# Pick steps dealt out anew, and six expert dots of units 8 and 9 on TensorE in place of five GpSimd products

## The reference, cut to what matters

```python
def peer_ffn(h, w_q, sub_keys, u_tab, v_tab):
    q = (xt @ w_q).reshape(n, PEER_HEADS, 2, PEER_QDIM // 2)
    s = jnp.einsum("nhpd,hpkd->nhpk", q, sub_keys)
    s1, i1 = lax.top_k(s[:, :, 0], PEER_TOPK)
    s2, i2 = lax.top_k(s[:, :, 1], PEER_TOPK)
    ...
    top_s, pos = lax.top_k(cand_s, PEER_TOPK)
    experts = jnp.take_along_axis(cand_i, pos, axis=-1)
    g = jax.nn.softmax(top_s, axis=-1)
    a = jax.nn.gelu(jnp.einsum("td,thkd->thk", xc, u_tab[ec]))
    return jnp.einsum("thk,thkd->td", gc * a, v_tab[ec])
```

## Time and profile before

| | us |
|---|---|
| median of 3 runs | 2062.68 (2062.55 to 2067.21) |
| profiled execution | 2062.78, span 2061.5 |
| early stage, first to last VectorE dot | 771.2 to 1304.5 |
| units 8 to 11 of it | 1134.6 to 1304.5 |
| spreading tile 1's coefficients | 1304.5 to 1339.0 |
| value stage | 1339.0 to 2061.5 |
| TensorE, VectorE, ScalarE, GpSimd busy | 1817.1, 1537.4, 868.2, 522.0 |

### The profile page before, as it was taken

The page is one execution under the profiler, slowest core; times in us unless marked ns, Lnnn a source line. Parts: engine busy times, 40 slices in busy tenths (PEclk is TensorE's granted clock), DMA queues, the critical chain, the costliest instruction groups (busy, mean ns, idle before and its releaser), DMA issues.

```text
span 2061.5 us, 28478 instructions
## 1 busy us (share of the span) xinstructions
PE 1817.1 (88%) x11068; PEld 1622.3 (79%) x11068; DVE 1537.4 (75%) x2053; ACT 868.2 (42%) x1347; POOL 522.0 (25%) x426
## 2 busy tenths in 40 slices
PE   6999999999999999957775244599999999999997
PEld 6999999999999887856775134488888888888886
DVE  5464444334465548999999989977888889999997
ACT  5444444444433441122332778534433444334443
POOL 0000000001044003433333577012121214443431
PEclk9999999999999999978898556799999999999999
DMA  9566555655466879999999899388999999999995
GB/s 313 160 169 174 163 163 169 174 166 164 143 181 218 312 252 419 380 423 384 394 384 396 305 427 427 124 310 332 417 400 386 401 376 378 407 395 405 397 409 187
DMA packets 293542, 627.87 MB, mean 305 GB/s; under 512 B 10364, under 2 KB 223405, under 8 KB 234958
## 3 DMA queue, kind: packets, MB, share of 16 engines
q0 software_dynamic: 48400, 343.95, 41.8%
q1 hardware_dynamic: 244558, 282.20, 40.0%
q10 hardware_dynamic: 496, 0.58, 0.1%
HBM read 622.45 MB, written 8.44 MB: 306 GB/s over the span
## 4 chain that ended last, share of the span: by engine, by line
PE 67%; DVE 16%; DVEq 7%; issue 4%; DMA 3%; POOL 2%; ACT 1%; SPq 0%; POOLq 0%; ACTq 0%
PE ps L1867 34%; PE ps L1553 23%; DVE u_ring L1398 7%; DVEq L1353 6%; PE ps L1733 4%; DMA u_ring<-in_peer_u,idx_all 2%; PE ps L1719 1%; POOL u_ring L667 1%; PE ps L1658 1%; PE ps L1639 1%; DVE ones L1430 1%; DVE ones_d L1430 1%; PE ps L1648 1%; DVE pick L1386 0%; DVE key_all L1389 0%
## 5 line engine op out<-in xcount | busy, mean ns | idle before, releaser
L1161 DVE TENSOR_TENSOR w_lo<-raw,w_hi 128x2048 fp32r<-128x2048 f32 x112 | 259.1, 2313 | 327.2 <-ACT w_hi L718 327.1
L1553 PE MATMUL ps<-act_hi,w_hi 128*128 128x256 f32 x1536 | 442.3, 288 | 4.8 <-DVE act_lo L1286 2.9
L1553 PE MATMUL ps<-act_hi,w_lo 128*128 128x256 f32 x1536 | 436.4, 284 | 0.0
L1553 PE MATMUL ps<-act_lo,w_hi 128*128 128x256 f32 x1536 | 436.4, 284 | 0.0
L1098 ACT ACTIVATE v_hi<-v_raw 128x2048 fp32r<-128x2048 f32 x128 | 245.5, 1919 | 404.0 <-PE ps L1867 211.4
L1867 PE MATMUL ps<-v_hi,c_hi 128*128 128x512 f32 x1024 | 404.6, 395 | 2.2 <-DVE c_lo L1481 2.2
L1867 PE MATMUL ps<-v_hi,c_lo 128*128 128x512 f32 x1024 | 403.2, 394 | 0.0
L1867 PE MATMUL ps<-v_lo,c_hi 128*128 128x512 f32 x1024 | 401.1, 392 | 0.0
L1398 DVE CUSTOM_DVE_ANT_0 u_ring<-u_ring,ps 128x2048 f32<-128x2048 f32 x156 | 353.9, 2277 | 21.4 <-DMA u_ring<-in_peer_u,idx_all 21.0
L1479 DVE TENSOR_TENSOR v_lo<-v_raw,v_hi 128x2048 fp32r<-128x2048 f32 x128 | 293.1, 2290 | 68.6 <-ACT v_hi L1098 67.5
L718 ACT ACTIVATE w_hi<-raw 128x2048 fp32r<-128x2048 f32 x112 | 214.1, 1911 | 266.8 <-PE ps L1553 222.0
(11 more groups left out here) (234 smaller groups left out, 2154.0 us busy)
## 6 DMA issues: line engine op xcount, KB each, us to landing
v_raw<-in_peer_v SPq DMA_DIRECT2D x128, 1024.0 KB
raw<-in_w_in SPq DMA_DIRECT2D x80, 1024.0 KB
raw<-in_w_out SPq DMA_DIRECT2D x16, 1024.0 KB
wq<-in_peer_w_q SPq DMA_DIRECT2D x8, 2048.0 KB, 12.7
raw<-in_w_br_a SPq DMA_DIRECT2D x16, 512.0 KB
bias_by_query<-bias_by_distance POOLq DMA_DIRECT2D x1, 4096.0 KB, 20.4
bias_st<-bias_by_query POOLq DMA_DIRECT2D x16, 256.0 KB, 4.7
raw<-in_w_br_b SPq DMA_DIRECT2D x16, 256.0 KB
```

Of the source, the lines that this page charges most:

```text
L1161: nc.vector.tensor_tensor(w_lo[:, j % NHL], raw[:, j % NRAW], w_hi[:, j % NHL].bitcast(F32), ALU.subtract).then_inc(lo_done, 1)
L1553: last = nc.tensor.matmul(out_ap, w_parts[wp][:, slot, k], act_parts[ap][:, k], start=(k == k0 and m == 0), stop=(k == k1 - 1 and m == 2))
```

## The change

It does four things.

1. **Six dots to TensorE.** In units 8 and 9 the picks (8, 1), (8, 5), (8, 9), (9, 0), (9, 4), (9, 8) (`PE_LATE`) go the way (c). The five picks there that GpSimd multiplied, (8, 7), (8, 12), (9, 2), (9, 7), (9, 12), go back to VectorE. All these late dots use PSUM banks 4 and 5 alone, since banks 0 to 3 hold the token rows: transposes alternate between the two, and the product goes into bank 4. So a late dot's transposes wait until VectorE has taken the diagonal of the dot before, the product waits for the third copied group, and ScalarE copies into one buffer (`rows_u`), where before there were two.
2. **Pick steps.** Unit 7 gets 18 steps in place of 26 and none in its last five picks, unit 8 gets 8 in place of 16 and only in its last six picks, unit 9 gets 16 in place of none.
3. **Coefficient groups.** ScalarE builds 21 in place of 18, seven in unit 8 (before 5), seven in unit 9 (before 5), six in unit 10 and one in unit 11. VectorE builds 11 in place of 14, none before unit 10, since their buffer lies over `xgT`, which the late dots read.
4. **Small things.** The identity scaled by the norm, by which the diagonal is taken, exists for both tiles; `slot_order` counts on a late TensorE dot's slot one pick later.

```diff
--- before.py
+++ after.py
@@ -86,10 +86,9 @@
 GROUPS = P // GTOK
 WQ_AT = (0, 16, 64, 80, 32, 48, 0, 16)
 WQ_TURN = tuple(WQ_AT[:u + 1].count(kib) for u, kib in enumerate(WQ_AT))
-ACT_GROUP_AT = {(8, 3): 0, (8, 5): 1, (8, 8): 2, (8, 11): 3, (8, 14): 4, (9, 1): 5, (9, 4): 6, (9, 7): 7, (9, 10): 8, (9, 13): 9,
-                (10, 1): 10, (10, 4): 11, (10, 7): 12, (10, 10): 13, (10, 13): 14, (11, 1): 15, (11, 3): 16, (11, 6): 17}
-DVE_GROUP_AT = {(9, 11): 0, (10, 0): 1, (10, 1): 2, (10, 5): 3, (10, 6): 4, (10, 10): 5, (10, 11): 6, (10, 15): 7,
-                (11, 1): 8, (11, 5): 9, (11, 6): 10, (11, 10): 11, (11, 11): 12, (11, 12): 13}
+ACT_GROUP_AT = {at: n for n, at in enumerate([(8, k) for k in (3, 4, 6, 8, 10, 12, 14)] + [(9, k) for k in (0, 2, 4, 7, 9, 11, 14)]
+                                             + [(10, k) for k in (0, 3, 5, 8, 11, 13)] + [(11, 1)])}
+DVE_GROUP_AT = {at: n for n, at in enumerate([(10, k) for k in (0, 1, 5, 6, 10, 11, 15)] + [(11, k) for k in (1, 5, 6, 10)])}
 ACT_GROUPS, DVE_GROUPS = len(ACT_GROUP_AT), len(DVE_GROUP_AT)
 W_INC = 48
 RING = 4
@@ -107,17 +106,20 @@
 
 
 EARLY = [(u, k) for u in range(N_EARLY) for k in range(PTOP)]
-STEPS_BY_UNIT = {0: 13, 1: 16, 2: 20, 8: 16, 9: 0, 10: 0, 11: 0}
+STEPS_BY_UNIT = {0: 13, 1: 16, 2: 20, 7: 18, 8: 8, 9: 16, 10: 0, 11: 0}
 
 
 def on_pool(u, k):
 
-    return u >= PH and k in (2, 7, 12) and (u, k) not in ((8, 2), (11, 12))
+    return u >= PH + 2 and k in (2, 7, 12) and (u, k) != (11, 12)
+
+
+PE_LATE = ((8, 1), (8, 5), (8, 9), (9, 0), (9, 4), (9, 8))
 
 
 def on_pe(u, k):
 
-    return 3 <= u < PH - 1 and k in (0, 3, 6, 9, 12) or u == PH - 1 and k in (0, 3, 5, 8) or u == 2 and k in (9, 12)
+    return 3 <= u < PH - 1 and k in (0, 3, 6, 9, 12) or u == PH - 1 and k in (0, 3, 5, 8) or u == 2 and k in (9, 12) or (u, k) in PE_LATE
 
 
 def quiet(u, k):
@@ -141,12 +143,13 @@
 
 
 EARLY_DOTS = dve_dots(N_EARLY, 0)
+PE_DOTS_0 = pe_dots(PH - 1, PTOP - 1)
 N_FEW = 2 * PTOP
 
 
 def slot_order():
 
-    freed = sorted(range(len(EARLY)), key=lambda n: n + (4.5 if on_pool(*EARLY[n]) else 3.5 if on_pe(*EARLY[n]) else 0))
+    freed = sorted(range(len(EARLY)), key=lambda n: n + (4.5 if on_pool(*EARLY[n]) else 3.5 + n // (PTOP * PH) if on_pe(*EARLY[n]) else 0))
     slots = []
     for n in range(len(EARLY)):
         if n < N_FEW:
@@ -165,7 +168,7 @@
 
     plan, done = {}, PICK_STEPS
     for u in range(N_EARLY):
-        open_at = [k for k in range(PTOP) if (3 <= k < 10 if u == 0 else not quiet(u, k) and not on_pe(u, k))]
+        open_at = [k for k in range(PTOP) if (3 <= k < 10 if u == 0 else not quiet(u, k) and not on_pe(u, k)) and (u != 7 or k < 11) and (u != 8 or k > 9)]
         count = STEPS_BY_UNIT.get(u, 26)
         for n, k in enumerate(open_at):
             upto = done + (n + 1) * count // len(open_at) - n * count // len(open_at)
@@ -266,8 +269,9 @@
     sc = at("sc", 160, [P, NU * 2 * PKEYS])
     ones = at("ones", 160, [P, 2, 2, GTOK, PKEYS])
     rows_t = at("rows_t", 32, [P, 2, NK, P])
-    diag_st = at("diag_st", 48, [P, P])
-    ident_r = at("ident_r", 48.5, [P, P])
+    rows_u = at("rows_u", 128, [P, NK, P])
+    diag_st = at("diag_st", 187, [P, P])
+    ident_r = at("ident_r", 187.5, [P, NT, P])
     ones_d = at("ones_d", 144, [P, 2, 2, GTOK, PKEYS])
     qp_st = at("qp_st", 176, [P, 2, T])
     sc_w = at("sc_w", 178, [P, 2, PKEYS])
@@ -1012,8 +1016,10 @@
             for g in range(4):
                 act.wait_ge(rt_pe, 4 * n + g + 1)
                 if g == 0:
-                    wait(act, mix_pe, n - 1)
-                nc.scalar.activation(rows_t[:, n % 2, 4 * g:4 * g + 4], ps[:, g % 2].rearrange("p (k t) -> p k t", k=4), ACT.Copy).then_inc(rt_ev, 1)
+                    wait(act, mix_pe, n - 1 if u < PH else n)
+                rows = rows_t[:, n % 2] if u < PH else rows_u
+                nc.scalar.activation(rows[:, 4 * g:4 * g + 4], ps[:, (4 if u >= PH else 0) + g % 2].rearrange("p (k t) -> p k t", k=4),
+                                     ACT.Copy).then_inc(rt_ev, 1)
 
         def picks_turned(tile):
             act.wait_ge(pk_pe, tile + 1)
@@ -1071,7 +1077,7 @@
             if k == 8 and c != PH:
                 tanh_of(c - 1)
             if (c, k) == (PH - 1, PTOP - 1):
-                act.wait_ge(diag_ok, pe_dots(PH, 0))
+                act.wait_ge(diag_ok, PE_DOTS_0)
                 act.wait_ge(xn2_ok, 1)
                 nc.scalar.activation(h2p[1], xg[:, 1], ACT.Copy).then_inc(hp_ok, 1)
             for u, step in PICK_PLAN.get((c, k), ()):
@@ -1402,7 +1408,7 @@
 
             n = pe_dots(u, k) - 1
             dve.wait_ge(mix_pe, n + 1)
-            nc.vector.tensor_tensor_reduce(out=diag_st[:, :], in0=ident_r[:, :], in1=ps[:, 2 + n % 2, 0:P], scale=0.5, scalar=0.0,
+            nc.vector.tensor_tensor_reduce(out=diag_st[:, :], in0=ident_r[:, u // PH], in1=ps[:, 4 if u >= PH else 2 + n % 2, 0:P], scale=0.5, scalar=0.0,
                                            op0=ALU.mult, op1=ALU.add, accum_out=early_dots[:, u, k:k + 1]).then_inc(diag_ok, 1)
 
         def gelu_argument(u):
@@ -1437,8 +1443,8 @@
             if k == 0 and c % PH == 0:
                 dve.wait_ge(hp_ok, c // PH + 1)
             if (c, k) == (2, 0):
-                dve.wait_ge(blk_done, N_WQ + 12)
-                nc.vector.tensor_scalar(ident_r[:, :], ident[:, :], stat[:, 3, 6:7], None, ALU.mult)
+                for t in range(NT):
+                    nc.vector.tensor_scalar(ident_r[:, t], ident[:, :], stat[:, 3, 6 + t:7 + t], None, ALU.mult)
             if not on_pool(c, k) and not on_pe(c, k):
                 dot(c, k)
             if on_pe(*EARLY[max(PTOP * c + k - 6, 0)]):
@@ -1788,22 +1794,29 @@
 
         def pe_dot(u, k):
 
-            n, slot = pe_dots(u, k) - 1, SLOT[PTOP * u + k]
+            n, slot, late = pe_dots(u, k) - 1, SLOT[PTOP * u + k], u >= PH
+            cols = slice(P * late, P * late + P)
             pe.wait_ge(u_in[slot], u_count(PTOP * u + k))
+            if late:
+                pe.wait_ge(diag_ok, n)
             for g in range(4):
                 wait(pe, rt_ev, 4 * n + g - 1)
                 for m in range(4):
-                    last = nc.tensor.transpose(ps[:, g % 2, P * m:P * m + P], u_ring[:, slot, P * (4 * g + m):P * (4 * g + m) + P], ident[:, :])
+                    last = nc.tensor.transpose(ps[:, 4 * late + g % 2, P * m:P * m + P], u_ring[:, slot, P * (4 * g + m):P * (4 * g + m) + P], ident[:, :])
                 last.then_inc(rt_pe, 1)
-            wait(pe, diag_ok, n - 1)
+            if late:
+                pe.wait_ge(rt_ev, 4 * n + 3)
+            else:
+                wait(pe, diag_ok, n - 1)
             for c in range(NK):
                 if c % 4 == 0:
                     pe.wait_ge(rt_ev, 4 * n + c // 4 + 1)
-                last = nc.tensor.matmul(ps[:, 2 + n % 2, 0:P], rows_t[:, n % 2, c], xgT[:, c, 0:P], start=(c == 0), stop=(c == NK - 1))
+                rows, bank = (rows_u, 4) if late else (rows_t[:, n % 2], 2 + n % 2)
+                last = nc.tensor.matmul(ps[:, bank, 0:P], rows[:, c], xgT[:, c, cols], start=(c == 0), stop=(c == NK - 1))
             last.then_inc(mix_pe, 1)
 
         for u, k in EARLY:
-            if on_pe(u, k):
+            if on_pe(u, k) and u < PH:
                 pe_dot(u, k)
 
         def turn_picks(tile):
@@ -1849,6 +1862,8 @@
                 dve_matrices(DVE_GROUP_AT[at_dot])
             if at_dot in ACT_GROUP_AT:
                 matrices(ACT_GROUP_AT[at_dot])
+            if at_dot in PE_LATE:
+                pe_dot(*at_dot)
         turn_picks(1)
         pe.wait_ge(dc_ev, DVE_GROUPS)
         for g in range(LATE_GROUPS):
```

## The result

The changed kernel takes **2084.43 us** (median of 4 runs, 2082.49 to 2085.29) beside 2062.61 us for the kernel before (4 runs, 2062.32 to 2067.21). The ratio is 1.0097, with a 95% interval of 1.0085 to 1.0109: slower by 21.8 us. The forecast was 2075.0 with a range of 2051 to 2090, so the sign and the range hold, and 9 us of the size are missing.

The account below looks back on a forecast made before the run. VectorE was taken to set the early stage's pace, waiting 10.0 us for data; TensorE fills the value stage. Plus 15.7 for ScalarE's list minus 3.1 behind it, plus 12.6 on 2062.8, gave 2075 us, range 2051 to 2090.

Parts of the forecast that it names:

- The step table: Units 7 to 9: moved pick steps fill unit 9's waits for gathers and could give 10.0 us back.
- ScalarE's list, plus 15.7: Units 8 and 9: ScalarE's queue holds the diagonal of (9, 8) until 1232.5, against 1216.8 before: plus 15.7 us.
- My 11 us of waits for TensorE: ScalarE's waits for TensorE ahead of (9, 8): 15 us at half clock, 7 at full, middle taken.
- Minus 3.1 behind that diagonal: Units 10 and 11: two VectorE groups gone, minus 4.0 us; one diagonal and one step added, plus 0.9.
- The change touches neither: Tile 1's coefficients (34.5 us) and value stage (722.5 us) unchanged; early stage's gain or loss reaches the end one to one.
- The clock: TensorE in units 8 and 9: above 0.6 under the forecast A, at 0.5 under rival D.
- the middle value: Between bounds of minus 3 and plus 29 us; plus 12.6 taken, citing a product of 5.37 us.
- Rival D: TensorE stays at half clock through units 8 and 9, 8.3 us per product: plus 26, 2089 us; chance 0.15.

Follow-up runs that it names:

- e1: Kernel before with the new pick-step table alone (18 in unit 7, 8 in unit 8, 16 in unit 9): 2060.01 us, ratio 0.9971.
- e12: Changed kernel with residual loads behind value blocks 44 and 80 and the final gains behind block 58: 2079.1 us, ratio 1.0071.
- e5: Changed kernel with residual loads behind value blocks 44 and 80 and the final gains behind block 100: 2081.42 us, ratio 1.0083.
- e3: Changed kernel with 18 ScalarE groups at about their old places and 14 VectorE groups, six late dots kept: 2072.5 us, ratio 1.0032.
- e4: Changed kernel with two late TensorE dots only, (8, 1) and (9, 8), the other four on VectorE: 2054.81 us, ratio 0.9941.

## Why the prediction was right, and where it was not

- **The step table**, "could give the 10.0 us back": e1 ended the early stage 10.2 us sooner. Dot (8, 0) was forecast at 1129.7 and started 1130.16.
- **ScalarE's list, plus 15.7**: the diagonal of (9, 8) was forecast at 1232.5 and started 1232.71, with 28.3 us of wait in all (forecast 20 to 35). Groups started 1139.18 (forecast 1139.9) and ScalarE reached (9, 8)'s copies at 1225.24 (forecast 1225). My 11 us of waits for TensorE were 12.5: 3.02 each ahead of (9, 0) and (9, 4), 2.86 and 3.64 at the `ct` copies after (8, 5) and (8, 9). The row sets took 2.4 to 2.8 us each with the short waits between their copies, where I had 2.8, and the groups began 0.7 us sooner than I had. So the terms are right to a microsecond or two, and that the sum met 1232.7 to 0.2 is luck: e12 and e5, with the same code up to there, have that diagonal at 1230.4 and 1227.9. ScalarE's share of the stretch was 77% (79.37 of 102.60 us), not over 85% as forecast. e3 and e4 show the mechanism, not only its date.
- **Minus 3.1 behind that diagonal did not come.** From there to the end of the early stage it took 87.6 us, where VectorE needed 87.8 from 1216.8 before. I had priced two groups at 4.0 and one step with one diagonal at 0.9. An undisturbed group takes 1.8 (0.68 for its first compare, 1.10 for the other four), so two are 3.6; and first compares that GpSimd holds up (below) took 1.7 us more in all than before, one of them 2.82. Together that is 1.8 off the busy time of the two lines (26.3 to 24.5). The pieces of a pick step that follow the diagonal were 0.69 + 0.69 + 0.17 = 1.6, and the diagonal 0.4. Minus 1.8 plus 2.0 is nothing. The size is within what two profiles of the same code differ by, so only the account by rows, not the end time, speaks for it.
- **"The change touches neither. What the early stage's end gains or loses reaches the end of the kernel one to one"** is the step that failed. The value stage took 7.3 us more. By rows: the hole, 3.27 us between two matmul starts that are usually 0.23 apart, 3.0; half clock for 3.4 us behind it, 1.7; the first 6.2 us of the stage at 0.50 where they had been at 0.72, 1.4; 1.2 are not accounted for. e12 takes the hole away and 5.3 us with it. The e1 run shows that the early end's gain is cut just as its loss was enlarged, so the term doesn't belong to the six dots: all six kernels here whose early stage was changed and whose loads stood at block 35 had a gap of 1.5 to 4.3 us there. Why the profiled execution of before escapes stays open; I did not vary the moment at which its value stage starts, and have no second profile of it.
- **The clock.** The average up to the diagonal of (9, 8) was 0.76, with pieces at either level (0.5 and 1.0); the products of late dots took 3.84 us three times and 5.09 to 5.47 three times. (The product of 5.37 us in the earlier trace rows, on which the middle value rested, ran at half clock from 1090.6 to 1094.0 and at full before and behind that; it didn't begin at half. The size was right all the same.) Rival D had 0.5 throughout and 8.3 per product, by my reading of "TensorE: Matmul & The Clock Gate", section "What's actually happening", in the Trainium skill. The page says that the half rate is the default and that sustained work releases it; that pieces between ScalarE's copies would never do so was my inference. The trace doesn't bear the inference out: at 1138.5, 1196.5 and 1213.6 the clock rose while ScalarE was copying the groups of (8, 1), (9, 0) and (9, 4).
- **Sum.** +15.7 in the early stage, -0.6 in the late matrices, +7.3 in the value stage, 22.4 of the span's 22.5. The forecast was 15.7 - 3.1 + 0. That the early stage's net loss equals the first of these terms is chance: the 3.1 failed, and one profile is good to some 5 us. The range held in spite of a missing term of 7.3 us because its upper end had been set for rival D.

## What to carry to other kernels

Before work is moved to an idle engine, follow every hand-over of it: a TensorE dot with a ScalarE copy in the middle is paced by ScalarE's in-order list, so six of them behind 12 coefficient groups cost VectorE 28 us, and two of them far apart nothing. A later stage that runs with its DMA queues full is not indifferent to its own rare loads: look for the place where a block is issued behind a large one-off transfer, try that transfer elsewhere (here blocks 44, 58 and 80 left no gap and blocks 35 and 100 did; what makes a place good is not shown), and don't count an earlier stage's gain one to one until that is done. And try the parts of a mixed change alone: here the table of numbers was the gain and the new data path the loss.
